# First-half low parts of six weight-sum pairs made on GpSimd in a two-block transformer kernel

## The chip, the cores and the metric

The kernel runs on one core of one Trainium2 chip. The metric is the device time of one execution in microseconds (us). Five engines matter: TensorE (PE in the profile, with its weight loads shown apart as PEld), VectorE (DVE), ScalarE (ACT), GpSimd (POOL) and SyncE (SP), which issues most DMAs. They run side by side, each through its own list of instructions in order, and wait for one another on semaphores.

## The reference, cut to what matters

The program computes two blocks on a sequence of 256 tokens of width 2048, all in float32: a conformer layer and a differential attention layer, then a hybrid layer with two kinds of attention. Nearly all the work is in products of activations with large weights:

```
u  = rms_norm(x) @ a_w_in            # 2048 x 6144
x  = x + y @ a_w_out                 # 2048 x 2048
kv = rms_norm(x, kv_norm_g) @ w_kv   # 2048 x 4096: K, then V
u  = rms_norm(x, norm_g) @ b_w_in    # 2048 x 4096: Q, then z
```

The change bears on the last 1024 columns of `w_kv` (half of V) and on the first 1024 columns of `b_w_in` (half of Q).

## The kernel before, in words

**Split precision.** TensorE multiplies float32 data in a fast rounded form (fp32r). To keep accuracy each operand is split in two: hi is the operand rounded by a copy, lo is the operand minus hi. A product is then three matmuls: hi·hi, hi·lo and lo·hi. ScalarE makes the hi part of each weight tile (line 637), VectorE the lo part by a subtraction (line 1133), from the tile that SyncE loaded into the ring `w_raw`. For units 18 to 91 GpSimd makes the lo parts instead (line 581), since VectorE has a convolution to do there.

**Units.** The weights are cut into chunks of 512 columns, and a chunk into units of 256 rows (two tiles of 128 x 512, together 128 x 1024). There are 426 units, and all engines walk them in the same order. A normal unit is 12 matmuls: two tiles, two halves of the tokens, three matmuls each. VectorE and ScalarE run about two units ahead of TensorE.

**Seven products for eight.** In two groups, chunks 22 and 23 (of `w_kv`) and chunks 24 and 25 (of `b_w_in`), the 2 x 2 block product of a unit of one chunk and the same unit of the next one is done with seven products instead of eight. It needs sums of the four weight tiles. There are six such pairs; their first units are 176, 180, 184, 188, 198 and 202, and this text calls them pairs 0 to 5. The second unit of pair 0 is 177, and so on. For each pair:

- VectorE makes the sums T1 and T3 (together "half 0", line 1147), then T2 (line 1150) and T4 (line 1151), together "half 1". This is `differences`.
- ScalarE makes the hi part of half 0 and then of half 1 (line 765).
- VectorE makes the lo part of half 0 and of half 1 (line 1156). This is `differences_lo`. It lies one step (one unit of VectorE's loop) apart: half 0 in front of the lo part of the pair's second unit, half 1 behind it.

The sums lie in different rooms: hi in `stage_r` or `heads_out_r`, the sums and their lo part in `aux` (named `aux_r` when written as fp32r), or in `room_a` and `actA_hi` for pair 4. The lo part overwrites the sum in place.

**What TensorE waits for in a pair.** In the first unit of a pair (`seven_products`): the lo part of that unit, then two products, 6 matmuls; then `third`, which needs the lo part of the pair's second unit and is 3 matmuls (pair 0 has it at the end of its second unit instead); then a wait for the lo part of half 0, and two products with half 0. In the second unit: a wait for half 1, and two products. Only the second tile of the pair's second unit is needed, so that unit's split is half as long (128 x 512).

**Order on VectorE around a pair**, as its loop has it: `differences` of the pair, the lo part of the pair's first unit, the lo part of half 0, the short lo part of the second unit, the lo part of half 1, and the lo parts of the next units. GpSimd has nothing to do in this part of the program: after the last line-581 instruction it waits until the attention at about 730 us.

**Lines that the steps touch:** 581 (GpSimd subtraction for `w_lo`), 637, 765, 1133, 1147, 1150, 1151, 1156, 1798 to 1800 (the three matmuls of a product in a pair), 1766 to 1768 (those of a normal unit), 1505 (a small VectorE instruction at 252 us).

Of the kernel before, what the change touches and what calls it, by code (L numbers as in the profile page):

```python
# [8 lines left out]
F32 = mybir.dt.float32  # L9
F32R = mybir.dt.float32r  # L10
ACT = mybir.ActivationFunctionType
ALU = mybir.AluOpType
# [59 lines left out]
for first in (C_OUT, C_OUTB):  # L72
    n = UNITS.index((first, 0))
    UNITS[n:n + 16] = [(first + c, 2 * g + i) for g in range(4) for c in range(2) for i in range(2)]
for g in SEVEN:
    n = UNITS.index((g["c"], 0))
# [12 lines left out]
SEVEN_AT = {u: n for n, u in enumerate(u for g in SEVEN for u in g["units"])}  # L89
# [172 lines left out]
moments_full moments_ready normed silu_ready x1_ready x1_kept x1_scale_ready x2_ready x2_scale_ready  # L262
lam_in lam_exp angle_ready sines_ready 
on_ready
sevens_whole sevens_acts sevens_acts_hi sevens_acts_lo sums_made sums_hi sums_lo sevens_first sevens_joined sevens_scaled
d_scores d_negmax d_exp d_probs d_pt d_pt_copied d_out d_gated
cq_scaled ckv_scaled kr_staged kr_roped qu_roped 
m_scores m_negmax m_exp m_probs m_pt m_pt_copied m_out m_out_copied
# [5 lines left out]
def hybrid_program(nc, t, out):  # L274
    with ExitStack() as ctx:
# [3 lines left out]
        S = {n: ctx.enter_context(nc.semaphore(n)) for n in SEMS}  # L279
# [170 lines left out]
        def sum_pair(n, half):  # L450
            return sum_room(n, half, False)

        def sum_pair_lo(n, half):
            return sum_room(n, half, True)

        def sum_pair_hi(n, half):
            if n % 2:
                return heads_out_r[:, 2 * half:2 * half + 2, :, :].rearrange("p a b c -> p (a b c)")
            return stage_r[:, half, :, :].rearrange("p a b -> p (a b)")
# [94 lines left out]
        @block.gpsimd  # L554
        def _(pool):
            chain = nc.gpsimd
            chain.memset(ident[:, :], 0.0).then_inc(S["ident_zero"], 1)
            pool.wait_ge(S["ident_zero"], 1)
            chain.affine_select(out=ident[:, :], in_=ident[:, :], compare_op=ALU.not_equal, fill=1.0,
                                base=0, pattern=[[-1, P]], channel_multiplier=1).then_inc(S["ident_ready"], 1)  # L560
            pool.wait_ge(S["ident_ready"], 1)
            chain.tensor_copy(ident_r[:, :], ident[:, :]).then_inc(S["ident_ready"], 1)
            chain.memset(strict[:, :], 1.0)
            chain.memset(neg_ones[:, :].bitcast(F32), -1.0)
            chain.memset(kr_t[:, :], 0.0)
            chain.memset(y_pad[:, :, 0:PAD], 0.0)
            inv_freq = np.float32(ROPE_THETA) ** (-np.arange(0, ROT, 2, dtype=np.float32) / np.float32(ROT))
            for i in range(ROT // 2):
                last = chain.memset(rope[:, 7, 0, i:i + 1], float(inv_freq[i]))
            last.then_inc(S["consts_ready"], 1)  # L570
            pool.wait_ge(S["consts_ready"], 1)
            chain.affine_select(out=strict[:, :], in_=strict[:, :], compare_op=ALU.is_gt, fill=0.0,
                                base=0, pattern=[[1, P]], channel_multiplier=-1)
            chain.affine_select(out=after[:, :], in_=neg_ones[:, :].bitcast(F32), compare_op=ALU.is_gt, fill=0.0,
                                base=0, pattern=[[-1, P]], channel_multiplier=1).then_inc(S["consts_ready"], 1)
            for u in range(SPLIT_AT[POOL_FROM], CONV_TO):
                for v in splits_at(u):
                    if LO_BY_POOL[v]:
                        w_part, w_rest = split_slot(v)
                        pool.wait_ge(S["w_hi_ready"], v + 1)  # L580
                        chain.tensor_tensor(w_rest, w_raw[:, RAW_SLOT[v], :], w_part.bitcast(F32), ALU.subtract)\  # L581
                            .then_inc(S["w_lo_pool"], 1)
                for j, m in [(j, m) for j, m, half in PAIRS_AT.get(u, []) if half]:
                    n = PAIR_FROM[j] + m
                    pool.wait_ge(S["products_ready"], n + 1)
                    chain.dma_start(pair_products(n, 0), pair_products(n, 1), accum_op=ALU.add)\
                        .then_inc(S[f"pair{n % SUMS}_summed"], 16)
            pool.wait_ge(S["d_scores"], HEADS)
            chain.memset(qr_t[:, :, :], 0.0).then_inc(S["rope_zero"], 1)  # L589
            pool.wait_ge(S["rope_zero"], 1)  # L590
            chain.memset(kr_t[64:65, 64:P], MASKED)
            chain.memset(kr_t[96:97, P + 64:SEQ], MASKED)
            chain.memset(qr_t[64:65, :, 0:64], 1.0)
            chain.memset(qr_t[96:97, :, P:P + 64], 1.0).then_inc(S["rope_padded"], 1)
# [508 lines left out]
        def _(dve):  # L1103
            n_chain = [0]
            V = nc.vector
# [44 lines left out]
                link(V.tensor_tensor(t2, b22, t1_t3[:, 0, :], ALU.subtract))  # L1150
                V.tensor_tensor(t4, b21, t2, ALU.subtract).then_inc(S["sums_made"], 1)

            def differences_lo(u, half):
                n = SEVEN_AT[u]
                dve.wait_ge(S["sums_hi"], 2 * n + half + 1)
                V.tensor_tensor(sum_pair_lo(n, half), sum_pair(n, half),
                                sum_pair_hi(n, half).bitcast(F32), ALU.subtract).then_inc(S["sums_lo"], 1)

            def seven_of_acts(n, step):

# [229 lines left out]
            for u, (c, s) in enumerate(UNITS):  # L1390
# [75 lines left out]
                        join_sevens(n, g, 1)  # L1466
                if u + 3 in SEVEN_AT:
                    differences(u + 3)
                if u + 2 in SEVEN_AT:
                    differences_lo(u + 2, 0)  # L1470
                if u + 1 in SEVEN_AT:
                    differences_lo(u + 1, 1)

                if u == SQUARES_AT[1]:
                    dve.wait_ge(S["x_squared"], 2)
# [191 lines left out]
        def _(pe):  # L1667
# [106 lines left out]
            def seven_products(u):  # L1774

                c, i = UNITS[u]
                g = SEVEN[IN_SEVEN[c]]
                second = c - g["c"]
                n, q = SEVEN_AT[u - second], g["quads"].index(i)
                kts, which = CHUNKS[c][3], g["which"]  # L1780
                opens, closes = q == 0, q == len(g["quads"]) - 1

                def act_parts(kk, tok):
                    k = kts[2 * i + kk]
                    return [part[which][:, k, tok * P:(tok + 1) * P] for part in (hi, lo)]

                def act_sums(m):
                    pairs = KEEP_PAIRS[g["kept"]]
                    return [part[:, m - 1, q, :] for part in (seven_acts_hi(pairs), seven_sums(aux_r, pairs))]

                def weight_parts(kk):
                    return [part[:, kk * NC:(kk + 1) * NC] for part in split_slot(u)]

                def weight_sums(half, m):
                    return [part[:, m * NC:(m + 1) * NC] for part in (sum_pair_hi(n, half), sum_pair_lo(n, half))]

                def one(bank, a, b, start, stop=False):
                    T.matmul(PS[:, bank, :], a[0], b[0], start=start, stop=False)  # L1798
                    T.matmul(PS[:, bank, :], a[0], b[1], start=False, stop=False)  # L1799
                    return T.matmul(PS[:, bank, :], a[1], b[0], start=False, stop=stop)  # L1800

                def third():
                    v = u + 1 - second
                    name_lo, n_lo = LO_READY[v]
                    pe.wait_ge(S[name_lo], n_lo)
                    return one(2, act_sums(4), [part[:, NC:2 * NC] for part in split_slot(v)], i == 0)

                name_lo, n_lo = LO_READY[u]
                if not second:
                    if i == 0:  # L1810
                        pe.wait_ge(S["chunk_read_act"], acts_up_to(c - 2))
                    if opens:
                        pe.wait_ge(S["t_copied"], COPY_NO["k3"] + 1)
                        pe.wait_ge(S["sevens_acts_lo"], g["kept"] + 1)
                    pe.wait_ge(S["lo_ready"], LO_NO[source[c, kts[2 * i + 1]]] + 1)
                    pe.wait_ge(S[name_lo], n_lo)
                    one(4, act_parts(0, 0), weight_parts(0), opens, closes)
                    one(0, act_parts(1, 0), weight_parts(1), i == 0)
                    if i:
                        third()  # L1820
                    pe.wait_ge(S["sums_lo"], 2 * n + 1)
                    one(7, act_sums(1), weight_sums(0, 0), opens, closes)
                    one(6, act_sums(3), weight_sums(0, 1), opens, closes).then_inc(S["units_done"], 1)
                else:
                    pe.wait_ge(S["sums_lo"], 2 * n + 2)
                    one(5, act_sums(2), weight_sums(1, 0), opens, closes)
                    ins = one(1, act_parts(1, 1), weight_sums(1, 1), i == 0)
                    if i == 0:
                        pe.wait_ge(S["chunk_read_act"], acts_up_to(c - 2))
                        ins = third()  # L1830
                    ins.then_inc(S["units_done"], 1)
# [304 lines left out]
```

## Time and profile before

| | |
|---|---|
| median of 3 runs | 1259.98 us (1259.84 to 1260.98) |
| the profiled execution's own time | 1260.29 us |
| its span, from the first to the last instruction | 1258.3 us |
| TensorE busy, share of the span | 99%, 5918 matmuls |
| VectorE busy | 833.7 us, 66% |
| ScalarE busy | 782.4 us, 62% |
| GpSimd busy | 204.8 us, 16% |
| TensorE on the chain of work that ended last | 96% |
| granted TensorE clock | 1.00 throughout |

The profile gives one execution. "Busy" is the time in which an engine had an instruction in work. A row of the timeline gives the start, the duration, the engine, the line, what is written and read, and in brackets how long the engine had been idle and who ended that. Rows of several instructions in a run are merged (x2, x3); their duration goes from the first start to the last end. Two records of an engine in a row overlap a little, since the next instruction starts while the last one still writes.

### The profile page before, as it was taken

Reading aid. Unit: us, or ns where it says so; the run is one execution under the profiler, and the core shown is the slowest. Engines: PE = TensorE matmul, PEld = TensorE weight load, DVE = VectorE, ACT = ScalarE, POOL = GpSimd, SP = SyncE. Lnnn points to the kernel's source line nnn. Section 1 sums busy time; section 2 is a strip of 40 time slices with the busy share of each in tenths; the row PEclk is TensorE's granted clock in tenths of the full one; section 3 lists DMA queues with packets and bytes.
Section 4 is the critical chain, followed back from the end, with each engine's and each line's share of the span. In section 5 each row is a group of like instructions: output and inputs, shape, how many; then the busy total and the mean of one; then the engine's idle time right before and its main releaser. Section 6 shows DMA issues by size and latency. Waiting matters only on the chain.

```text
span 1258.3 us, 16105 instructions
## 1 busy us (share of the span) xinstructions
PE 1248.2 (99%) x5918; PEld 1039.5 (83%) x5918; DVE 833.7 (66%) x1341; ACT 782.4 (62%) x1230; POOL 204.8 (16%) x149
## 2 busy tenths in 40 slices
PE   9999999999999999999999999999999999999998
PEld 7888888888888888778888888889988888888886
DVE  5497898476657667898787765656544445576545
ACT  5798798765547556555667674456644454666543
POOL 1499999900000000000000010000000000000000
PEclk9999999999999999999999999999999999999999
DMA  9899998944556566666555455566655556655553
GB/s 347 271 255 252 269 254 244 270 161 142 183 194 183 189 185 183 200 189 213 156 162 156 151 164 192 186 185 173 186 166 159 160 158 186 193 164 159 184 193 133
DMA packets 133564, 243.85 MB, mean 194 GB/s; under 512 B 12144, under 2 KB 22512, under 8 KB 133360
## 3 DMA queue, kind: packets, MB, share of 16 engines
q1 hardware_dynamic: 129600, 229.40, 58.7%
q0 software_dynamic: 3600, 13.11, 5.3%
q8 instruction: 48, 0.79, 0.3%
q10 hardware_dynamic: 288, 0.32, 0.1%
q14 instruction: 28, 0.23, 0.1%
HBM read 227.60 MB, written 2.10 MB: 183 GB/s over the span
## 4 chain that ended last, share of the span: by engine, by line
PE 96%; DVE 2%; ACT 1%; DMA 0%; issue 0%; SPq 0%; DVEq 0%; ACTq 0%
PE PS L1766 29%; PE PS L1768 29%; PE PS L1767 28%; PE PS L1685 2%; PE PS L1704 2%; PE PS L1798 1%; PE PS L1799 1%; PE PS L1800 1%; PE PS L1952 1%; DMA w_raw<-in_a_w_in 0%; PE PS L1848 0%; PE PS L1850 0%; PE PS L1849 0%; PE PS L2044 0%; PE PS L2014 0%; DVE w_lo L1133 0%
## 5 line engine op out<-in xcount | busy, mean ns | idle before, releaser
L1133 DVE TENSOR_TENSOR w_lo<-w_raw,w_hi 128x1024 fp32r<-128x1024 f32 (+2 forms) x339 | 407.8, 1204 | 302.9 <-ACT w_hi L637 302.2
L637 ACT ACTIVATE w_hi<-w_raw 128x1024 fp32r<-128x1024 f32 (+2 forms) x383 | 399.2, 1044 | 335.0 <-PE PS L1768 303.5
L1766 PE MATMUL PS<-w_hi,actB_hi 128*128 128x512 f32 (+1 forms) x736 | 292.4, 397 | 0.7 <-DVE aux L1196 0.7
L1768 PE MATMUL PS<-w_hi,actB_lo 128*128 128x512 f32 (+1 forms) x736 | 284.8, 387 | 0.0
L1767 PE MATMUL PS<-w_lo,actB_hi 128*128 128x512 f32 (+1 forms) x736 | 284.1, 386 | 0.0
L1766 PE MATMUL PS<-w_hi,actA_hi 128*128 128x512 f32 x724 | 283.6, 392 | 0.0
L1768 PE MATMUL PS<-w_hi,actA_lo 128*128 128x512 f32 x724 | 282.2, 390 | 0.0
L1767 PE MATMUL PS<-w_lo,actA_hi 128*128 128x512 f32 x724 | 281.8, 389 | 0.0
L1768 PEld LDWEIGHTS PS<-w_hi,actB_lo 128*128 128x128 f32 x736 | 138.1, 188 | 28.8
L1766 PEld LDWEIGHTS PS<-w_hi,actB_hi 128*128 128x128 f32 x736 | 138.3, 188 | 26.4 <-DVE aux L1196 1.1
L1768 PEld LDWEIGHTS PS<-w_hi,actA_lo 128*128 128x128 f32 x724 | 135.9, 188 | 28.9
L1767 PEld LDWEIGHTS PS<-w_lo,actB_hi 128*128 128x128 f32 x736 | 138.4, 188 | 25.6
L1767 PEld LDWEIGHTS PS<-w_lo,actA_hi 128*128 128x128 f32 x724 | 136.0, 188 | 27.9
L1766 PEld LDWEIGHTS PS<-w_hi,actA_hi 128*128 128x128 f32 x724 | 135.9, 188 | 28.0 <-DVE actA_lo L1211 0.3
L581 POOL TENSOR_TENSOR w_lo<-w_raw,w_hi 128x1024 fp32r<-128x1024 f32 x44 | 124.3, 3172 | 0.0
L1324 DVE SCALAR_TENSOR_TENSOR PS<-aux,PS 128x256 f32<-128x256 f32 x264 | 104.5, 480 | 0.0
L581 POOL TENSOR_TENSOR w_more<-w_raw,w_more 128x1024 fp32r<-128x1024 f32 x30 | 85.6, 3150 | 46.0 <-ACT w_more L637 46.0
L1089 ACT ACTIVATE tap_products<-aux 128x256 f32<-128x256 f32 x200 | 84.6, 499 | 0.1
L589 POOL MEMSET aux<- 128x2048 f32 x1 | 1.8, 1820 | 475.2 <-PE PS L1704 475.2
L637 ACT ACTIVATE w_more<-w_raw 128x1024 fp32r<-128x1024 f32 x36 | 37.9, 1057 | 20.8 <-PE PS L1768 20.4
L1766 PE MATMUL PS<-w_more,actA_hi 128*128 128x512 f32 x128 | 50.8, 397 | 0.0
L1768 PE MATMUL PS<-w_more,actA_lo 128*128 128x512 f32 x128 | 50.2, 392 | 0.0
(336 smaller groups left out, 1256.3 us busy)
## 6 DMA issues: line engine op xcount, KB each, us to landing
w_raw<-in_a_w_in SPq DMA_DIRECT2D x95, 512.0 KB, 5.8
w_raw<-in_w_in SPq DMA_DIRECT2D x88, 512.0 KB, 3.7
w_raw<-in_w_kv SPq DMA_DIRECT2D x64, 512.0 KB, 3.8
w_raw<-in_b_w_in SPq DMA_DIRECT2D x64, 512.0 KB, 3.8
w_raw<-in_a_w_out SPq DMA_DIRECT2D x32, 512.0 KB, 3.8
w_raw<-in_b_w_out SPq DMA_DIRECT2D x32, 512.0 KB, 3.7
w_raw<-in_w_out SPq DMA_DIRECT2D x32, 512.0 KB, 4.3
tap_products<-tap_products POOLq DMA_DIRECT2D x25, 512.0 KB, 8.3
```

The costliest lines, as they stand in the source:

```text
L581: chain.tensor_tensor(w_rest, w_raw[:, RAW_SLOT[v], :], w_part.bitcast(F32), ALU.subtract)\
L637: nc.scalar.activation(split_slot(u)[0][:, f:2 * w], w_raw[:, RAW_SLOT[u], f:2 * w], ACT.Copy)\
L1089: ins = nc.scalar.activation(pair_products(n, i)[:, k - 4 * j, :], y_pad[:, k, tap:tap + SEQ], ACT.Copy, scale=taps[:, k, tap:tap + 1])
L1133: V.tensor_tensor(wl, w_raw[:, RAW_SLOT[u], f:2 * w], wh.bitcast(F32), ALU.subtract)\
L1324: ins = V.scalar_tensor_tensor(tap_sums(i) if kind == "tap" else conv[:, k, :], y_pad[:, k, tap:tap + SEQ], taps[:, k, tap:tap + 1], tap_s ...
L1685: return T.transpose(out.bitcast(F32R), src, ident_r[:, :])
L1704: ins = T.matmul(PS[:, bank, f:e], q[:, q0:q0 + P], k[:, 0:e - f], start=f == 0 and i == 0, stop=f == P and i == len(pairs) - 1)
L1766: T.matmul(bank, ah, wh[:, kk, :], start=(first or opens_last and tok == 1) and kk == 0, stop=False)
L1767: T.matmul(bank, ah, wl[:, kk, :], start=False, stop=False)
L1768: ins = T.matmul(bank, al, wh[:, kk, :], start=False, stop=last and kk == 1)
L1798: T.matmul(PS[:, bank, :], a[0], b[0], start=start, stop=False)
L1799: T.matmul(PS[:, bank, :], a[0], b[1], start=False, stop=False)
```

## The change

GpSimd gets a loop of six subtractions, placed behind its last `w_lo` and in front of its wait for the attention: the lo part of half 0 of each pair. Each waits for the second half of the sums (`sums_made`, since T2 reads T1 out of the room that is overwritten) and for the hi part of half 0 (`sums_hi`). VectorE keeps the lo part of half 1 only. TensorE waits for half 0 on a new semaphore.

```
+            for n in range(len(SEVEN_AT)):
+                pool.wait_ge(S["sums_made"], 2 * n + 2)
+                pool.wait_ge(S["sums_hi"], 2 * n + 1)
+                chain.tensor_tensor(sum_pair_lo(n, 0), sum_pair(n, 0), sum_pair_hi(n, 0).bitcast(F32), ALU.subtract)\
+                    .then_inc(S["sums_lo_pool"], 1)
             pool.wait_ge(S["d_scores"], HEADS)
...
-            def differences_lo(u, half):
+            def differences_lo(u):
                 n = SEVEN_AT[u]
-                dve.wait_ge(S["sums_hi"], 2 * n + half + 1)
-                V.tensor_tensor(sum_pair_lo(n, half), sum_pair(n, half),
-                                sum_pair_hi(n, half).bitcast(F32), ALU.subtract).then_inc(S["sums_lo"], 1)
+                dve.wait_ge(S["sums_hi"], 2 * n + 2)
+                V.tensor_tensor(sum_pair_lo(n, 1), sum_pair(n, 1),
+                                sum_pair_hi(n, 1).bitcast(F32), ALU.subtract).then_inc(S["sums_lo"], 1)
...
-                if u + 2 in SEVEN_AT:
-                    differences_lo(u + 2, 0)
                 if u + 1 in SEVEN_AT:
-                    differences_lo(u + 1, 1)
+                    differences_lo(u + 1)
...
-                    pe.wait_ge(S["sums_lo"], 2 * n + 1)
+                    pe.wait_ge(S["sums_lo_pool"], n + 1)
                     one(7, act_sums(1), weight_sums(0, 0), opens, closes)
                     one(6, act_sums(3), weight_sums(0, 1), opens, closes).then_inc(S["units_done"], 1)
                 else:
-                    pe.wait_ge(S["sums_lo"], 2 * n + 2)
+                    pe.wait_ge(S["sums_lo"], n + 1)
```

On VectorE, around pair 0, the list before reads (the three sums, then the lo part of unit 176, half 0, unit 177, half 1, and units 178 and 179):

```order
L1147 TENSOR_TENSOR aux<-w_raw 128x1024
L1150 TENSOR_TENSOR aux<-w_raw,aux 128x512
L1151 TENSOR_TENSOR aux<-w_raw,aux 128x512
L1133 TENSOR_TENSOR w_lo<-w_raw,w_hi 128x1024
L1156 TENSOR_TENSOR aux_r<-aux,stage_r 128x1024
L1133 TENSOR_TENSOR w_lo<-w_raw,w_hi 128x512
L1156 TENSOR_TENSOR aux_r<-aux,stage_r 128x1024
L1133 TENSOR_TENSOR w_lo<-w_raw,w_hi 128x1024 x2
```

and now, with the line numbers shifted by five:

```order
L1152 TENSOR_TENSOR aux<-w_raw 128x1024
L1155 TENSOR_TENSOR aux<-w_raw,aux 128x512
L1156 TENSOR_TENSOR aux<-w_raw,aux 128x512
L1138 TENSOR_TENSOR w_lo<-w_raw,w_hi 128x1024
L1138 TENSOR_TENSOR w_lo<-w_raw,w_hi 128x512
L1161 TENSOR_TENSOR aux_r<-aux,stage_r 128x1024
L1138 TENSOR_TENSOR w_lo<-w_raw,w_hi 128x1024 x2
```

One subtraction is gone from between the lo parts of the pair's two units; half 1 stays behind them.

On GpSimd, behind the last lo parts of the early units, the list now reads (line 591 is new, line 594 is the first instruction of the attention):

```order
L581 TENSOR_TENSOR w_lo<-w_raw,w_hi 128x1024 x2
L591 TENSOR_TENSOR aux_r<-aux,stage_r 128x1024
L591 TENSOR_TENSOR aux_r<-aux,heads_out_r 128x1024
L591 TENSOR_TENSOR aux_r<-aux,stage_r 128x1024
L591 TENSOR_TENSOR aux_r<-aux,heads_out_r 128x1024
L591 TENSOR_TENSOR actA_hi<-room_a,stage_r 128x1024
L591 TENSOR_TENSOR aux_r<-aux,heads_out_r 128x1024
L594 MEMSET aux 128x2048
```

The six rows of line 591 are pairs 0 to 5 in order; before, the row of the memset followed the row of line 581.

## Rows read from the trace of the kernel before

**Rows 1.** The page, part 1: busy us, share of the span, count.

```profile
PE 1248.2 (99%) x5918; PEld 1039.5 (83%) x5918; DVE 833.7 (66%) x1341; ACT 782.4 (62%) x1230; POOL 204.8 (16%) x149
```

**Rows 2.** Stretch 500 to 580 us: PE, PEld, DVE, ACT, POOL, clock, DMA share, GB/s.

```profile
500.00:580.00 80.00, 79.19 (x345) 64.03 (x345) 69.87 (x76) 46.39 (x49) 0.00 (x0) 1.00 0.65 197
```

**Rows 3.** Waits of TensorE's weight loads, 500 to 580 us: total, times, longest.

```profile
PEld PS L1798 <- DVE w_lo L1133: 1.1, 4, 0.5
```

**Rows 4.** Timeline of VectorE, pair 3: start, duration, line, out<-in.

```profile
533.06 0.69 DVE L1151 TENSOR_TENSOR aux<-w_raw,aux 128x512 f32<-128x512 f32 x1
533.67 1.22 DVE L1133 TENSOR_TENSOR w_lo<-w_raw,w_hi 128x1024 fp32r<-128x1024 f32 x1
534.80 1.22 DVE L1156 TENSOR_TENSOR aux_r<-aux,heads_out_r 128x1024 fp32r<-128x1024 f32 x1
535.94 0.68 DVE L1133 TENSOR_TENSOR w_lo<-w_raw,w_hi 128x512 fp32r<-128x512 f32 x1
```

**Rows 5.** Timeline of ScalarE, pair 3.

```profile
532.33 1.06 ACT L765 ACTIVATE heads_out_r<-aux 128x1024 fp32r<-128x1024 f32 x1 [1.06 <-DVE aux L1147]
534.75 0.61 ACT L637 ACTIVATE w_hi<-w_raw 128x512 fp32r<-128x512 f32 x1
```

**Rows 6.** Timeline of the weight loads: start of `third`, pairs 1 to 5.

```profile
516.04 0.19 PEld L1798 LDWEIGHTS PS<-w_hi,aux_r 128*128 128x128 f32 x1 [0.46 <-DVE w_lo L1133]
...
526.41 0.19 PEld L1798 LDWEIGHTS PS<-w_hi,aux_r 128*128 128x128 f32 x1 [0.29 <-DVE w_lo L1133]
...
536.68 0.19 PEld L1798 LDWEIGHTS PS<-w_hi,aux_r 128*128 128x128 f32 x1 [0.20 <-DVE w_lo L1133]
...
564.14 0.19 PEld L1798 LDWEIGHTS PS<-w_hi,aux_r 128*128 128x128 f32 x1
564.37 0.19 PEld L1799 LDWEIGHTS PS<-w_lo,aux_r 128*128 128x128 f32 x1
...
574.49 0.19 PEld L1798 LDWEIGHTS PS<-w_hi,aux_r 128*128 128x128 f32 x1 [0.19 <-DVE w_lo L1133]
```

**Rows 7.** Timeline of VectorE, pair 0, and the short split of pair 4.

```profile
501.80 0.69 DVE L1151 TENSOR_TENSOR aux<-w_raw,aux 128x512 f32<-128x512 f32 x1
502.41 1.22 DVE L1133 TENSOR_TENSOR w_lo<-w_raw,w_hi 128x1024 fp32r<-128x1024 f32 x1
...
505.28 1.22 DVE L1156 TENSOR_TENSOR aux_r<-aux,stage_r 128x1024 fp32r<-128x1024 f32 x1
...
563.33 0.68 DVE L1133 TENSOR_TENSOR w_lo<-w_raw,w_hi 128x512 fp32r<-128x512 f32 x1
```

**Rows 8.** Timeline of the weight loads, pair 0: first loads with half 0, half 1.

```profile
505.05 0.19 PEld L1798 LDWEIGHTS PS<-stage_r,aux_r 128*128 128x128 f32 x1
...
506.55 0.19 PEld L1798 LDWEIGHTS PS<-stage_r,aux_r 128*128 128x128 f32 x1 [0.17 <-DVE aux_r L1156]
```

**Rows 9.** Line 581 on GpSimd: ns min/median/max, then two rows of its timeline.

```profile
L581 POOL TENSOR_TENSOR w_lo<-w_raw,w_hi x44: 2407/3166/4124, 54.6 to 251.3; 128x1024 fp32r<-128x1024 f32 x44
...
54.56 7.14 POOL L581 TENSOR_TENSOR w_lo<-w_raw,w_hi 128x1024 fp32r<-128x1024 f32 x3
61.65 2.43 POOL L581 TENSOR_TENSOR w_more<-w_raw,w_more 128x1024 fp32r<-128x1024 f32 x1
```

**Rows 10.** Timelines of VectorE and GpSimd at 250 us, and VectorE at 40 us.

```profile
252.21 2.49 DVE L1505 TENSOR_SCALAR st<-st 128x2 f32<-128x2 f32 x1
...
248.77 5.89 POOL L581 TENSOR_TENSOR w_lo<-w_raw,w_hi 128x1024 fp32r<-128x1024 f32 x2
...
40.39 0.17 DVE L1232 TENSOR_SCALAR st<-st 128x2 f32<-128x2 f32 x1 [0.48 <-ACT aux L786]
```

**Rows 11.** Line 1324 on VectorE, beside GpSimd's line 581: ns min/median/max.

```profile
L1324 DVE SCALAR_TENSOR_TENSOR PS<-aux,PS x264: 468/480/492, 63.2 to 223.9; 128x256 f32<-128x256 f32 x132
```

**Rows 12.** Timelines of VectorE and GpSimd at 49 us.

```profile
48.74 1.23 DVE L1133 TENSOR_TENSOR w_lo<-w_raw,w_hi 128x1024 fp32r<-128x1024 f32 x1 [0.84 <-ACT w_hi L637]
...
49.74 4.86 POOL L581 TENSOR_TENSOR w_more<-w_raw,w_more 128x1024 fp32r<-128x1024 f32 x2 [45.19 <-ACT w_more L637]
```

More of the change, by code:

```diff
@@ L264 @@
 on_ready
-sevens_whole sevens_acts sevens_acts_hi sevens_acts_lo sums_made sums_hi sums_lo sevens_first sevens_joined sevens_scaled
+sevens_whole sevens_acts sevens_acts_hi sevens_acts_lo sums_made sums_hi sums_lo sums_lo_pool sevens_first sevens_joined sevens_scaled
 d_scores d_negmax d_exp d_probs d_pt d_pt_copied d_out d_gated
```

## The prediction

> **What bounds the kernel now.** I read the page first: TensorE is busy for 1248.2 of the 1258.3 us of the span [rows 1]. So the time is TensorE's own work plus its few holes, and an engine beside it counts only where TensorE waits for it. Next the stretch of the six pairs, 500 to 580 us: TensorE busy 79.19 of 80 us, VectorE 69.87 (87%), GpSimd 0.00 [rows 2]. Then the waits of the weight loads there: 1.1 us in four waits for `w_lo` (line 1133) [rows 3], and 0.17 us in one, in pair 0, for the lo part of half 1 (line 1156) [rows 8]. The reader is to see two things. All that a freed VectorE can give back is about 1.3 us, 0.1% of the time. And VectorE in this stretch does almost nothing but subtractions with both inputs in SBUF, the large memory, which is also what GpSimd is to do now beside it.
>
> **The change, part by part.** VectorE loses six instructions of 1.22 us, which follow one another at 1.13 us (534.80 to 535.94 in pair 3) [rows 4]. GpSimd gains six of the same shape. TensorE's matmuls are the same. No DMA is added or moved past another; GpSimd's new waits have only the attention's memset behind them, some 150 us later.
>
> *Length of the new instruction.* Line 581 has the same form, 128x1024 minus 128x1024. Its records last 2.41 to 4.12 us, but records in a row overlap: three fill 7.14 us and the next begins 7.09 us after the first, so one takes 2.36 us of the engine, and an isolated one 2.41 [rows 9]. I take 2.41.
>
> *When it can start.* Pair 3 stands for all. T4 ends at 533.06 + 0.69 = 533.75 [rows 4], the hi part of half 0 at 532.33 + 1.06 = 533.39 [rows 5]. GpSimd is released at about 533.8, when VectorE has just begun the lo part of unit 188 (533.67 to 534.89) [rows 4].
>
> *What the two engines do to each other.* This decides the forecast, and no row has a long VectorE subtraction under a long GpSimd one. The nearest rows: at 252.21 us a VectorE instruction on two elements (line 1505), in SBUF only, took 2.49 us; its like at 40.39 took 0.17. It ended at 254.70, and GpSimd's last subtraction at 248.77 + 5.89 = 254.66 [rows 10]. Two elements can't need 2.3 us: VectorE stood still until GpSimd's whole instruction was over. Against that, line 1324, with one input in SBUF and one in PSUM, ran beside line 581 in 468 to 492 ns, undisturbed [rows 11]. The VectorE work in the pairs is on line 1505's side: it has no operand in PSUM. One place has an overlap of the right kind: GpSimd began at 49.74 while line 1133 ran until 49.97 [rows 12]; two instructions took 4.86 us against 2.36 + 2.43 by the other rows, 0.07 more, which an exclusion or nothing could give. So the bounds for one pair are no effect and full exclusion, each instruction holding the other off until it ends. I take full exclusion, by line 1505.
>
> The Trainium skill, in "SBUF — State Buffer", section "Who interferes with whom", says that a VectorE instruction with two SBUF inputs contends with a GpSimd one that reads SBUF, and that the first to start holds the shared ports for the whole instruction. Line 1505's wait agrees; for subtractions with two inputs no row here shows it. By this rule the result is the forecast below, and it is the rule that speaks against the change.
>
> *One pair under exclusion.* GpSimd waits for VectorE until 534.89. VectorE's next instruction, the short lo part of unit 189, has lost the one in front of it, but its hi part is ready only at 534.75 + 0.61 = 535.36 [rows 5]. In that gap GpSimd gets the memory and keeps it until 534.89 + 2.41 = 537.30. VectorE then makes the short lo part, 0.68, to 537.98. Before it ended at 535.94 + 0.68 = 536.62 [rows 4]: 1.36 later, and with two handovers that are not hidden, some 0.04, 1.4. `third` waits for it, and already waited before: its row has the bracket at 536.68 [rows 6]. So TensorE pays all 1.4 us. Half 0 is ready at 537.30, ahead of `third`, so the new wait costs nothing itself. Half 1 follows the short part by 1.1 us, and TensorE has 9 matmuls to do until then, at 0.23 us each (564.14 to 564.37 [rows 6]): covered.
>
> - Pairs 1, 2, 3, 5: `third` waited in each (idle 0.46, 0.29, 0.20, 0.19 [rows 6]), so each adds the full 1.4: 5.6 us.
> - Pair 4: `third` started at 564.14 without a wait; its lo part was ready at 563.33 + 0.68 = 564.01 [rows 6, 7]. 0.13 is free: 1.27 us.
> - Pair 0 has no `third` in its first unit. VectorE ends unit 176 at 503.63, GpSimd at 506.04; TensorE wanted half 0 at 505.05 [rows 7, 8]: a stall of 1.0. Then VectorE makes the short part (0.6 until the next can start) and half 1 (1.22): 507.86, where it was 506.50 before and where TensorE already waited [rows 7, 8]. 1.36 and a handover: 1.4 us in all, the 1.0 within it.
>
> Sum: 5.6 + 1.27 + 1.4 = 8.3 us. Nothing behind gives it back: loads, hi parts and sums of the next pair all follow TensorE's or VectorE's own lateness, so each pair begins in the same position relative to TensorE. Of the profiled execution that makes 1260.29 + 8.3 = 1268.6 us; its 1260.29 is 0.3 over the median 1259.98, so **1268.3 us** by the median, 0.66% slower.
>
> **Rivals.**
>
> *No contention: not slower.* For it: line 1324 undisturbed [rows 11], and an overlap at 49.74 that cost 0.07 at most [rows 12]. Then GpSimd works 533.8 to 536.2 and VectorE has 1.13 us more room before the short lo part. The waits at `third` go, less 0.04 each that lie between any two loads (0.19 long, 0.23 apart [rows 6]): 0.42 + 0.25 + 0.16 + 0.15 = 1.0. In pair 0 half 1 comes early and its 0.13 goes; half 0 there comes at 502.55 + 2.41 = 504.96 against 505.05, just in time. 1260.29 − 1.1 = 1259.2, by the median 1258.9. It decides if a GpSimd subtraction stays at 2.4 us beside line 1133. Against it: line 1505 [rows 10].
>
> *The ports are shared element by element.* Neither stands still, both get slower. At half speed for both in the overlap, the lo part of unit 188 ends about 536.0 instead of 534.9, the short one of 189 about 537.3 instead of 536.62, and half 0 about 538.6, where TensorE, having begun `third` at 537.3, wants it at 538.0. That is about 0.7 + 0.6 us a pair, 7 to 8 in all: nearly the forecast. If they slow each other by a third of that, some 2.5 us: 1262.5. I put its middle at 1264. Against it: line 1505 got nothing at all done for 2.3 us.
>
> *Exclusion and more.* The lateness of VectorE frees the `w_raw` ring later; each pair's sums then wait for their load. The price is taken from the longest wait of the stretch, 0.5 us [rows 3], once in four of the pairs: 2 us, 1270.3. For it: the ring refills only behind the lo parts, which get later. Against: TensorE is as late as the loads are.
>
> *The change does not do what it says:* excluded as far as order goes; the six instructions stand on GpSimd in an idle stretch. The one way is that GpSimd gets no turn until VectorE has idled twice; the gap of 0.47 us (534.89 to 535.36) argues against that, and TensorE would then pay at half 0 instead, over 1.4 us a pair.
>
> **How the numbers follow.** Exclusion 0.68, exclusion and more 0.08, shared 0.12, no contention 0.12. What a measurement of this kernel can tell from no change is about 0.2%, 2.5 us: 1257.5 to 1262.5. Faster by more needs over 2.5 us, and all of TensorE's waits in the stretch are 1.3: 0.02. No contention, and a third of the shared case, lie within 0.2%: 0.16. Slower: 0.82. The forecast's own range is 1266.5 to 1270, from a handover of 0 to 0.15 us and a GpSimd instruction of 2.3 to 2.5 us in six pairs. The range for 8 in 10 goes from 1261.5, leaving out no contention and a little of the shared case, to 1271.
>
> **What would show it.** In the profile after: the records of line 591 on GpSimd of 2.4 us, or of 3.5 with the wait for VectorE in them; the short lo part (line 1138, 128x512) ending 4.4 us after the start of the unit's lo part, or lasting some 2.5 instead of 0.68 us; TensorE's waits at `third` of 1.3 to 1.9 us in five pairs, put down to `w_lo`, and two waits in pair 0; 500 to 580 us stretched by 8 us; nothing new outside it. The forecast is wrong if line 1138 keeps 1.22 and 0.68 us with GpSimd busy beside it, or if `third` does not wait.

## The result, and the profile after

The changed kernel takes **1265.18 us** (median of 6 runs, 1265.01 to 1265.49) against 1260.12 for the kernel before (6 runs, 1259.84 to 1260.98). The ratio is 1.004, 95% interval 1.0029 to 1.005: 3.7 to 6.3 us slower. Forecast was 8.3 us slower, 1268.3. Direction and mechanism held; the size was too large by 3.2 us. The profiled execution took 1265.07 us, its span is 1263.1, 4.8 more than before.

The page after, part 1, answers to [rows 1]. TensorE has the same 5918 matmuls, VectorE six instructions fewer and yet 3.7 us more busy time, GpSimd six more and 20.0 us more:

```profile
span 1263.1 us, 16111 instructions
PE 1249.3 (99%) x5918; PEld 1039.6 (82%) x5918; DVE 837.4 (66%) x1335; ACT 782.4 (62%) x1230; POOL 224.8 (18%) x155
```

Six VectorE subtractions of 1.22 us are gone and its busy time rises: something there must have been standing still. The waits of the weight loads, 500 to 585 us, after (who waited, for whom, total, times, longest), against [rows 3]:

```profile
PEld PS L1801 <- DVE w_lo L1138: 5.4, 5, 1.3
PEld PS L1769 <- DVE aux L1201: 1.1, 1, 1.1
PEld PS L1801 <- POOL aux_r L591: 0.9, 1, 0.9
PEld PS L1801 <- DVE aux_r L1161: 0.5, 1, 0.5
```

The second row is TensorE's wait for VectorE's joining of the products behind the first group, 1.1 us before too. The others went from 1.1 + 0.2, and 0.46 more in pair 1's first unit that the profile put to issue, to 6.8. That wait of 0.46 is not in [rows 3]:

```profile
514.36 0.19 PEld L1798 LDWEIGHTS PS<-w_hi,actA_hi 128*128 128x128 f32 x1 [0.46 <-issue]
```

Five of the seven other waits are for `w_lo`, not for GpSimd. Pair 3 shows why. The timeline of VectorE after, against [rows 4]:

```profile
534.77 0.69 DVE L1156 TENSOR_TENSOR aux<-w_raw,aux 128x512 f32<-128x512 f32 x1
535.38 1.22 DVE L1138 TENSOR_TENSOR w_lo<-w_raw,w_hi 128x1024 fp32r<-128x1024 f32 x1
537.11 2.30 DVE L1138 TENSOR_TENSOR w_lo<-w_raw,w_hi 128x512 fp32r<-128x512 f32 x1 [0.51 <-ACT w_hi L642]
539.33 1.21 DVE L1161 TENSOR_TENSOR aux_r<-aux,heads_out_r 128x1024 fp32r<-128x1024 f32 x1
```

and the timeline of GpSimd and of the weight loads after, against [rows 6]:

```profile
535.54 3.32 POOL L591 TENSOR_TENSOR aux_r<-aux,heads_out_r 128x1024 fp32r<-128x1024 f32 x1 [8.02 <-DVE aux L1156]
...
539.46 0.19 PEld L1801 LDWEIGHTS PS<-w_hi,aux_r 128*128 128x128 f32 x1 [1.26 <-DVE w_lo L1138]
```

Read it so. GpSimd is released at 535.54, while VectorE makes the lo part of unit 188 until 536.60. GpSimd's record ends at 538.86: 3.32 us long, of which 1.06 is the wait for VectorE and 2.26 its hold, in which VectorE gets nothing done. VectorE's short subtraction is issued in that time, at 537.11, and ends at 539.41: 2.30 us for work that takes 0.68, 0.55 after GpSimd's end. From the start of the unit's lo part to the end of the short one it was 2.95 us and is 4.03, 1.08 more, and `third` waits 1.26 instead of 0.20.

Pair 0 has the two waits that were forecast, against [rows 8]:

```profile
505.84 0.19 PEld L1801 LDWEIGHTS PS<-stage_r,aux_r 128*128 128x128 f32 x1 [0.91 <-POOL aux_r L591]
...
507.52 0.19 PEld L1801 LDWEIGHTS PS<-stage_r,aux_r 128*128 128x128 f32 x1 [0.46 <-DVE aux_r L1161]
```

And `third` in pairs 1, 2, 4 and 5:

```profile
516.79 0.19 PEld L1801 LDWEIGHTS PS<-w_hi,aux_r 128*128 128x128 f32 x1 [0.57 <-DVE w_lo L1138]
...
528.12 0.19 PEld L1801 LDWEIGHTS PS<-w_hi,aux_r 128*128 128x128 f32 x1 [1.26 <-DVE w_lo L1138]
...
567.93 0.19 PEld L1801 LDWEIGHTS PS<-w_hi,aux_r 128*128 128x128 f32 x1 [1.04 <-DVE w_lo L1138]
...
579.27 0.19 PEld L1801 LDWEIGHTS PS<-w_hi,aux_r 128*128 128x128 f32 x1 [1.26 <-DVE w_lo L1138]
```

The waits after less those before, pair by pair, each bracket less the 0.04 that lie between any two loads: +1.2, −0.3 (the two waits of 0.46 in pair 1 before, against one of 0.57), +1.0, +1.1, +1.0, +1.1. Before rounding the sum is 4.95 us. The spans of the two traces differ by 4.8, and at 500 us the execution after was 0.1 us ahead; the medians differ by 5.1. Pair 1 is the odd one.

### The profile page after: what moved, and what is told of

It reads as the page before. It is cut to its first block, busy times and chain, and to the rows that moved or that the text cites. A ratio compares the mean times of both kernels' runs of the same rounds, so it can differ in the third digit from the quotient of the medians.

```text
span 1263.1 us, 16111 instructions
## 1 busy us (share of the span) xinstructions
PE 1249.3 (99%) x5918; PEld 1039.6 (82%) x5918; DVE 837.4 (66%) x1335; ACT 782.4 (62%) x1230; POOL 224.8 (18%) x155
## 4 chain that ended last, share of the span: by engine, by line
PE 90%; DVE 5%; ACT 2%; issue 1%; DMA 1%; DVEq 0%; SPq 0%; ACTq 0%
PE PS L1769 27%; PE PS L1771 27%; PE PS L1770 27%; PE PS L1688 2%; DVE w_lo L1138 2%; PE PS L1707 2%; ACT w_hi L642 1%; PE PS L1955 1%; DVE aux L1152 0%; PE PS L1801 0%; PE PS L1851 0%; PE PS L1853 0%; DMA w_raw<-in_b_w_in 0%; PE PS L1852 0%; PE PS L1803 0%
## 5 line engine op out<-in xcount | busy, mean ns | idle before, releaser
L1138 DVE TENSOR_TENSOR w_lo<-w_raw,w_hi 128x1024 fp32r<-128x1024 f32 (+2 forms) x339 | 417.6, 1233 | 305.4 <-ACT w_hi L642 304.6
L591 POOL TENSOR_TENSOR aux_r<-aux,stage_r 128x1024 fp32r<-128x1024 f32 x2 | 6.6, 3319 | 256.0 <-DVE aux L1156 256.0
```

Of the source, the lines that this page charges most:

```text
L591: chain.tensor_tensor(sum_pair_lo(n, 0), sum_pair(n, 0), sum_pair_hi(n, 0).bitcast(F32), ALU.subtract)\
L1138: V.tensor_tensor(wl, w_raw[:, RAW_SLOT[u], f:2 * w], wh.bitcast(F32), ALU.subtract)\
```

## The experiments

The theory after the result: **exclusion.** A subtraction of GpSimd and one of VectorE that both read two inputs from SBUF don't run at the same time; each waits for the other's whole instruction. Its rival: GpSimd is merely slow, and TensorE waits for its result. A second question was pair 1. The first four rows of the table are compared with one group of 27 runs of the kernel before (median 1260.01 us), the last four with another (median 1260.47). Five of the eight have 1 in their interval: by its time alone none of them can be told from the kernel before.

| experiment | median us | ratio to before, 95% interval |
|---|---|---|
| spare GpSimd subtraction, nobody waits | 1268.95 | 1.0067 (1.0053 to 1.0082) |
| spare GpSimd writes, nobody waits | 1260.39 | 1.0001 (0.9992 to 1.001) |
| change in pair 0 alone | 1260.89 | 1.0006 (0.9997 to 1.0015) |
| short lo part first, no GpSimd | 1259.66 | 0.9997 (0.9988 to 1.0006) |
| GpSimd subtraction of half the width | 1262.67 | 1.0019 (1.001 to 1.0028) |
| change in pair 3 alone | 1261.27 | 1.0007 (0.9998 to 1.0016) |
| GpSimd released later | 1275.21 | 1.0118 (1.0104 to 1.0132) |
| short lo part first, again | 1259.6 | 0.9995 (0.9986 to 1.0004) |

### A spare subtraction that nobody waits for

```
+            for n in range(len(SEVEN_AT)):
+                pool.wait_ge(S["sums_made"], 2 * n + 2)
...
+                chain.tensor_tensor(flat_work[:, 0:768], x_res[:, 0, 0:768], x_res[:, 1, 0:768], ALU.subtract)\
+                    .then_inc(S["spare"], 1)
```

> The kernel before, all lo parts on VectorE, with a spare GpSimd subtraction beside each pair: 128x768, both inputs from x_res (not the data of the pair), result into a buffer that nobody reads; nothing waits for it until the attention. It separates contention from the new dependency. Exclusion theory: a VectorE subtraction (1.22 us before) now shows one record per pair longer by about the length of the GpSimd instruction (0.75 of 2.26, 1.7 us), the short lo part ends 1.1 to 1.7 us later and TensorE waits at third by that much: 1266 to 1270 us, if GpSimd gets its turn between two VectorE instructions that follow without a gap. If GpSimd only gets in where VectorE idles, its record lasts 3 us or more, it starts behind half 1, and the time stays within 1 us of before. Rival (the cost of the change is only that GpSimd is slow and TensorE waits for it): no VectorE record changes, 1260.1 +- 0.3.

Measured: 1268.95 us, 8.9 more than before, though GpSimd's result is never used and VectorE has all its work of before. The waits of the weight loads, 500 to 600 us, without the join, went from 1.8 to 10.3 us, and the span by 8.6:

```profile
PEld PS L1806 <- DVE w_lo L1139: 8.3, 5, 1.9
PEld PS L1806 <- DVE aux_r L1162: 2.0, 2, 1.4
```

The timelines of VectorE and GpSimd in pair 3 of this kernel:

```profile
537.52 1.22 DVE L1139 TENSOR_TENSOR w_lo<-w_raw,w_hi 128x1024 fp32r<-128x1024 f32 x1
538.66 2.88 DVE L1162 TENSOR_TENSOR aux_r<-aux,heads_out_r 128x1024 fp32r<-128x1024 f32 x1
541.46 0.68 DVE L1139 TENSOR_TENSOR w_lo<-w_raw,w_hi 128x512 fp32r<-128x512 f32 x1
...
537.68 2.77 POOL L592 TENSOR_TENSOR work<-x_res 128x768 f32<-128x768 f32 x1 [9.16 <-DVE aux L1157]
```

GpSimd waits until VectorE's running instruction ends (538.74) and then gets its turn at once, though VectorE's next one is ready with no gap. It holds it until 540.45, and line 1162 lasts 2.88 instead of 1.22 us; it is so in all six pairs. The rival's 1260.1 is out. The Trainium skill, "SBUF — State Buffer", section "Summary: rules for kernel authors", says of a VectorE instruction with two SBUF inputs and a GpSimd one that reads SBUF that the second to issue fully blocks until the first has finished; this run agrees, 1.66 us on one instruction.

### Spare writes instead of a subtraction

```
+                for i in range(3):
...
+                    chain.memset(flat_work[:, 0:768], float(i)).then_inc(S["spare"], 1)
```

> As the run before, but GpSimd writes instead of subtracting: three memsets of 128x768 in the same buffer at the same places, reading nothing; about 0.7 us each. Exclusion only between instructions that both read SBUF: no VectorE record changes, 1260.1 +- 0.3. If any GpSimd work in SBUF holds VectorE's subtractions off: 1262 to 1266.

Measured: 1260.39, ratio 1.0001: no difference. GpSimd was in work for 2.35 us beside each pair, and VectorE's records kept their length (both timelines, pair 3):

```profile
534.19 2.35 POOL L593 MEMSET work<- 128x768 f32 x3 [7.92 <-DVE aux L1157]
...
535.18 1.22 DVE L1162 TENSOR_TENSOR aux_r<-aux,heads_out_r 128x1024 fp32r<-128x1024 f32 x1
```

So GpSimd's being busy in SBUF is not enough: an instruction of it that only writes holds nothing off, and what the subtraction has besides is its reading of two inputs. A GpSimd instruction with one input was not run.

### The change in pair 0 alone

```
-            for n in range(len(SEVEN_AT)):
+            for n in POOL_PAIRS:      # [0]
...
+                if u + 2 in SEVEN_AT and SEVEN_AT[u + 2] not in POOL_PAIRS:
+                    differences_lo(u + 2, 0)
```

> The changed kernel with only pair 0's half 0 on GpSimd; pairs 1 to 5 as before. Theory (pair 1 gives back what pair 0 costs, because its first and third waits of 0.42 and 0.42 us came from a load that landed late, and TensorE being late hides both): pair 0 costs 1.16, pair 1 returns 0.8, sum +0.3: 1260.4. Rival (that load landed late by chance in one execution): +1.2 us, 1261.3. My prediction's step: +1.4, 1261.5.

Measured: 1260.89, ratio 1.0006 with 1 in its interval; the time can't tell +0.3 from +1.2. The trace shows where the cost went in one execution. Its waits of the weight loads, 500 to 580 us:

```profile
PEld PS L1772 <- DVE aux L1202: 1.1, 1, 1.1
PEld PS L1804 <- POOL aux_r L592: 0.9, 1, 0.9
PEld PS L1804 <- DVE w_lo L1139: 0.7, 3, 0.3
PEld PS L1804 <- DVE aux_r L1162: 0.5, 1, 0.5
```

The three waits for `w_lo` are those of pairs 2, 3 and 5; pair 1 has none at all. Against the trace of the kernel before, pair 0's 1.2 us more are met by 0.8 less in pair 1, and the span is 1258.5 against 1258.3. But the profiled execution is the fastest of the 11 (1260.34 us). The median is 0.9 us above the kernel before, between the two expectations of +0.3 and +1.2.

Part of the reason is the load for which pair 1's sums wait, that of unit 181. Its row of the view of `w_raw`, from its issue to its last piece, before and here:

```profile
DMA to landing us min/median/max: 5.0/5.0/5.0
```
```profile
DMA to landing us min/median/max: 3.7/3.7/3.7
```

The short lo part frees its slot and comes later here, so the load is issued 2.8 us behind the one in front of it instead of 1.7. Over the traces of all kernels the second load of a pair took 4.4 to 5.1 us at a spacing of 1.2, 4.1 to 5.0 at 1.7, 4.1 to 4.4 at 2.3, 3.6 to 3.7 at 2.8 and 3.6 to 3.8 at 3.4. So the load makes up the delay of its issue, while TensorE is late in any case.

The other part is chance. The spare writes and the change in pair 3 alone leave pairs 0 and 1 as they were, and there the same load, at the same spacing of 1.7 us, took 4.4 and 4.6 us instead of 5.0. VectorE's first sum of pair 1 in the kernel before, with the spare writes, with the change in pair 3 alone and in the changed kernel:

```profile
510.44 1.22 DVE L1147 TENSOR_TENSOR aux<-w_raw 128x1024 f32<-128x1024 f32 x1 [1.22 <-DMA w_raw<-in_w_kv]
510.66 1.23 DVE L1153 TENSOR_TENSOR aux<-w_raw 128x1024 f32<-128x1024 f32 x1 [0.66 <-DMA w_raw<-in_w_kv]
511.14 1.22 DVE L1153 TENSOR_TENSOR aux<-w_raw 128x1024 f32<-128x1024 f32 x1 [0.85 <-DMA w_raw<-in_w_kv]
510.11 1.23 DVE L1152 TENSOR_TENSOR aux<-w_raw 128x1024 f32<-128x1024 f32 x1 [0.19 <-DMA w_raw<-in_w_kv]
```

TensorE's waits in pair 1 were 0.84 us in the first, and only 0.18 and 0.37 in the two others without the change there. So the one trace of the kernel before caught a late landing. Against the other two, pair 1 of the changed kernel (0.53) costs 0.35 or 0.16 us more, not 0.3 less. It also fits the time of the run with pair 0 alone: 1.2 us less waits of 0.2 to 0.8 is +0.3 to +1.0, and 0.9 was measured.

### The change in pair 3 alone

> The changed kernel with only pair 3's half 0 on GpSimd. By the trace of the changed kernel pair 3 costs 1.07 us (a wait at third of 1.23 in place of 0.16), and nothing behind it gives that back: 1261.1, and the gap at the join of the sums behind pair 3 stays 1.1 us. If a following stage gives it back as pair 1 did for pair 0: 1260.2. My prediction's term was 1.4: 1261.5.

The edit is that of the run before with `[3]`. Measured: 1261.27, ratio 1.0007, 0.8 us more than before, with 1 just inside the interval. The profiled execution is the slowest of the 11: 1.0 us of the 2.0 us by which its span is longer lies in front of 500 us. Behind that, the trace gives the short lo part of pair 3 with 2.29 us and `third` with 1.35 us over the normal step instead of 0.16: +1.2 us, and the 1.1 at the join behind it stays. Nothing gives a pair's cost back there; the size agrees with the theory, though the time alone doesn't prove a difference.

### Half the width

```
-                chain.tensor_tensor(sum_pair_lo(n, 0), sum_pair(n, 0), sum_pair_hi(n, 0).bitcast(F32), ALU.subtract)\
+                chain.tensor_tensor(sum_pair_lo(n, 0)[:, NC:2 * NC], sum_pair(n, 0)[:, NC:2 * NC],
+                                    sum_pair_hi(n, 0)[:, NC:2 * NC].bitcast(F32), ALU.subtract)\
...
+                if u + 2 in SEVEN_AT:
+                    first_lo(u + 2)          # the other 512 columns, on VectorE
```

> The changed kernel with GpSimd's subtraction cut to half, 128x512 (the T3 half), and the T1 half of half 0 back on VectorE, where the whole half 0 was before. Exclusion theory, with GpSimd getting its turn at the first boundary between two VectorE instructions: the T1 part's record lasts 0.55 after a hold of about 1.15 us, 1.7 us in all; the short lo part ends 0.5 us later than before the change; waits at third of 0.6 to 0.7 us in pairs 2, 3 and 5, 0.4 in pair 4, about 0.5 in pair 0, none or little in pair 1: 1262.0, between the two kernels. If the hold had a fixed cost and were not in proportion to the instruction's length: as the changed kernel, 1265. Rival (only slowness of GpSimd counts): half 0 is ready in time and the time is that of before, 1260.

Measured: 1262.67, ratio 1.0019 (1.001 to 1.0028), 2.2 us more than before, between the two kernels as exclusion had it. TensorE waited 0.67 us at `third` in pair 1 too, where none or little was expected. VectorE and GpSimd in pair 3:

```profile
534.75 1.22 DVE L1139 TENSOR_TENSOR w_lo<-w_raw,w_hi 128x1024 fp32r<-128x1024 f32 x1
535.89 1.79 DVE L1162 TENSOR_TENSOR aux_r<-aux,heads_out_r 128x512 fp32r<-128x512 f32 x1
...
534.91 2.22 POOL L591 TENSOR_TENSOR aux_r<-aux,heads_out_r 128x512 fp32r<-128x512 f32 x1 [8.65 <-DVE aux L1157]
```

GpSimd's hold is 537.13 − 535.97 = 1.16 us for 512 columns. With 1.71 for 768 (the spare subtraction) and 2.26 for 1024 it is 0.06 us and 2.15 ns a column: in proportion, with almost no fixed part. All three had waited 1.06 us in their records before; that time got GpSimd nothing done.

### GpSimd released later

```
                 pool.wait_ge(S["sums_hi"], 2 * n + 1)
+                pool.wait_ge(S["w_lo_ready"], LO_READY[list(SEVEN_AT)[n] + 1][1])
```

> The changed kernel, but GpSimd waits in addition for the short lo part of the pair's second unit, so that it can't hold that one off. Exclusion theory: GpSimd is released when VectorE has just begun half 1, waits for its end, and holds the memory from about 537.1 to 539.4 in pair 3's terms; the waits at third go, but TensorE, which wants half 0 at about 537.1, waits 2.2 us for it: per pair 2.0 to 2.2 us more than before in pairs 1 to 5 and 3 us in pair 0: 1269 to 1272, worse than the changed kernel. Rival (no exclusion, GpSimd takes 2.4 us from its release): half 0 at 538.5, a wait of 1.3 us: 1266.

Measured: 1275.21, 14.7 more than before; both expectations are missed: exclusion had 9 to 12 more, its rival 6. The waits are exclusion's: all waits at `third` are gone, the short part is 0.69 us long again, and TensorE waits 10.8 + 2.1 us for GpSimd in six waits, 11.1 us more than it waited in the pairs before. The first is 3.19 us long, and with it something new happens. The weight loads, and two stretches with busy time (PE, PEld, DVE, ACT, POOL), granted clock, DMA share and GB/s:

```profile
508.28 0.29 PEld L1802 LDWEIGHTS PS<-stage_r,aux_r 128*128 128x128 f32 x1 [3.19 <-POOL aux_r L592]
508.44 0.33 PEld L1803 LDWEIGHTS PS<-aux_r 128*128 128x128 f32 x1
508.87 0.33 PEld L1804 LDWEIGHTS PS<-stage_r,aux_r 128*128 128x128 f32 x1
...
508.00:514.50 6.50, 6.22 (x15) 4.90 (x16) 3.41 (x3) 1.06 (x1) 0.23 (x1) 0.51 0.35 107
514.50:522.00 7.50, 7.50 (x35) 6.08 (x33) 5.17 (x7) 4.54 (x5) 2.75 (x1) 1.00 0.62 179
```

From 508.4 to 514.4 us the granted clock is about a half, the 1.2 GHz level, and a load comes every 0.43 us instead of 0.23; TensorE had stood still before in the wait. It happens once more, for some 3.4 us from 548.5 on (clock 0.50), behind the wait of 2.31 us in pair 3, but not behind those of 2.31 in pairs 2 and 5 and of 2.11 in pair 4. Some 20 steps of 0.43 instead of 0.23 us are about 4 us which neither theory had. With the new operand the last to come, the change cost 14.7 us instead of 5.1.

### The short lo part first

```
-                if u + 2 in SEVEN_AT:
-                    differences_lo(u + 2, 0)
                 if u + 1 in SEVEN_AT:
+                    if SEVEN_AT[u + 1]:
+                        differences_lo(u + 1, 0)
                     differences_lo(u + 1, 1)
```

(pair 0 keeps its order.)

> The kernel before, nothing on GpSimd, with the order on VectorE changed in pairs 1 to 5: the lo part of half 0 behind the short lo part of the pair's second unit instead of in front of it. Theory (TensorE's waits at third are waits for the short lo part only): these waits, 0.42 + 0.25 + 0.16 + 0.15 us, go, and half 0 comes just in time (in pair 3 at about 537.2, wanted at 537.2): 1259.1, about 0.08% faster than before, at worst the same if half 0 is late by 0.1 to 0.2 us in each pair. Rival (the waits come from elsewhere): 1260.1.

> The kernel of the run that puts half 0 behind the short lo part on VectorE, again, for its time: its trace has 1.1 us less of holes in 500 to 580 us than before; its time was 0.35 us less, within the interval. Expected 1259.0 to 1259.7 against 1260.0. If the ratio again includes 1, what stays is that the holes go and the time can't tell.

Measured: 1259.66 and 1259.6 us, 0.35 and 0.87 less than before, ratios 0.9997 and 0.9995, both with 1 in the interval. The traces show less waiting, each for one execution. In the first run the waits of the weight loads in 500 to 580 us are down to the join alone:

```profile
PEld PS L1768 <- DVE aux L1196: 1.1, 1, 1.1
```

and its span is 1257.3. In the second the load of unit 181 landed later (VectorE idle 1.10 us for it, against 0.64 in the first), waits of 0.33 and 0.35 us stood in pair 1 and one of 0.18 in pair 0, and the span was 1257.8. So that pair 1 of the first run has no wait is owed to the load in part. That the waits of [rows 6] in pairs 2, 3 and 5 were waits for the short lo part is shown, since they are gone in both traces; that this order is faster isn't, by the times.

## Why the prediction was right, and where its size was off

- **What bounds it.** Right: the difference is the sum of TensorE's holes in 500 to 585 us, 4.95 us in the traces against 5.1 by the medians. The prediction's count of the waits before, 1.3 us, left out the 1.1 at the join and the 0.46 in pair 1 that the profile put to issue. The second mattered, see below.
- **Exclusion, taken from line 1505 [rows 10].** Right, and shown apart from everything else: a spare subtraction with a hold of 1.71 us stretches a VectorE one by 1.66, three writes of 2.35 us in all stretch none. The step from line 1505 to a subtraction was a guess that came true. Line 1505 has one tensor as input, not two, so it can't bear out a rule for two inputs; and "no operand in PSUM" is not the dividing line: just before it VectorE ran two instructions with one input, all in SBUF, in 0.39 us together while GpSimd was in work [rows 10]:

```profile
251.79 0.39 DVE L1503 BATCH_NORM_AGGREGATE st<-st 128x2 f32<-128x24 f32 x2
```

- **The gap in which GpSimd gets its turn.** Right in the changed kernel (536.60 to 537.11 in pair 3), but the reasoning was not needed: in the spare run GpSimd got it between two instructions with no gap.
- **Waits land on `w_lo` at `third`, two in pair 0, none for half 0 elsewhere.** Right in all six pairs. Each sign came smaller than forecast: 3.32 us for line 591 instead of 3.5, 4.03 to the end of the short part instead of 4.4, waits at `third` of 0.57 to 1.26 instead of 1.3 to 1.9.
- **One pair costs 1.4 us: mis-sized.** It measured 1.0 to 1.1 in pairs 2 to 5. The hold was 2.26 us where the prediction took GpSimd's isolated record of 2.41, 0.15 less. The short subtraction ended 0.55 us after the hold, not 0.68: 0.13 less. The handovers of 0.04 did not show. 1.4 − 0.15 − 0.13 − 0.04 = 1.08. That the start of an instruction is what both durations lost, since it lay in the wait, fits but was not tried. Over pairs 2 to 5 it makes 5.47 − 4.1 = 1.4 us of the error of 3.3 by the traces. Pair 0 was 1.2 instead of 1.4, another 0.2.
- **"Nothing behind gives it back": the step that failed.** It failed in pair 1, forecast at +1.4, measured −0.3, 1.7 us of the 3.3. The argument that each pair begins in the same position holds only where the pair waits for something that is delayed along with it. Pair 1 before was held up by a load: VectorE stood idle 1.22 us for it, and two waits of 0.46 followed. With pair 0 late, the load was issued 1.0 us later and took 1.3 less. Some 0.5 to 0.65 us of the 1.7 are chance, since two other executions without the change in pairs 0 and 1 waited only 0.18 and 0.37 us there; against them pair 1 cost +0.35 and +0.16, still over 1 us short of the forecast. That the spacing of the loads causes the give-back rests on their landing times against the spacing over all traces. It was not tried by itself, and the time of the run with pair 0 alone doesn't decide it.
- **Rivals.** No contention is refuted by the trace and by the spare run. Sharing element by element too: VectorE's 1.22 us stayed 1.22 with GpSimd waiting beside it, GpSimd's hold behind it was in full proportion to its columns, and the short subtraction ended 0.55 us after that hold, about what it takes when alone. "Exclusion and more", later loads, went the other way.

## What to carry to other kernels

GpSimd was no free engine for elementwise work with two SBUF inputs beside a VectorE that does the same: the work moved cost VectorE GpSimd's time (2.26 us held) instead of its own (1.13 us saved), whoever waits for the result. Before moving such work, look at the kind of operands VectorE has in that stretch, not at GpSimd's idle share: with a PSUM operand on VectorE [rows 11], or with writes alone on GpSimd, nothing was held off. For VectorE instructions with one SBUF input the runs don't settle it: line 1505 was held, line 1503 was not. Where a stall is added in front of a pair that waited for a load, that wait can absorb part of it. And a hole of a microsecond seen in one trace may differ by half a microsecond in the next execution of the same kernel, so look at a second trace before a forecast or an explanation rests on it.

## What the runs showed of the hardware that was not expected

- GpSimd gets its turn at the first end of a VectorE instruction, even in an unbroken row of them: 538.74 in the spare run, where VectorE's next record begins at 538.66.
- The hold of a GpSimd subtraction is 0.06 us and 2.15 ns a column (1.16, 1.71, 2.26 us for 512, 768, 1024).
- In the kernel with the late release, waits of TensorE of 3.19 and 2.31 us were followed by stretches at about half the granted clock (0.51 in 508.0 to 514.5), some 4 of its 14.7 us. Two other waits of 2.31 us and one of 2.11 were not.
- The second of a pair's two 512 KB loads took 3.6 to 3.8 us when it was issued 2.8 us or more behind the first, and 4.1 to 5.1 when 2.3 us or less behind.
